# Latent attention: the queries' root mean square as a scale per row of the softmax, and steps of pairs in another order

## The reference, cut to what matters

```python
def _rmsnorm(x, g):
    y = x * lax.rsqrt(mean(x * x, axis=-1) + RMS_EPS)
    return y * g

def _mla_branch(x, w_in, q_norm, w_q_up, kv_norm, w_kv_up, w_out):
    h = x @ w_in                                   # 384 q, 256 kv, 32 rope, 1024 gate
    cq, ckv, k_rope, gate = split(h)
    q  = _rmsnorm(cq, q_norm) @ w_q_up             # 16 heads of 64 + 32 (rope)
    kv = _rmsnorm(ckv, kv_norm) @ w_kv_up          # 16 heads of 64 (k) + 64 (v)
    q_rope, k_rope = rope(q[..., 64:]), rope(k_rope)
    s = (q_full @ k_full.T) * 96 ** -0.5           # causal
    o = softmax(s) @ v
    return (o * silu(gate)) @ w_out

x = layernorm((2 * DEPTH) ** 0.25 * x + y)         # after each of the four layers
```

## Time and profile before

| What | Value |
|---|---|
| median of three runs | 1652.9 us (1652.37 to 1653.56) |
| profiled execution, its own time | 1657.83 us |
| its span, first to last instruction | 1656.0 us |
| mean granted TensorE clock | 0.995 |
| PE matmul busy | 1620.8 us (98%) |
| DVE, ACT, POOL busy | 776.0, 757.8, 658.2 us |
| share of PE in the chain that ended last | 80% |

### The profile page before, as it was taken

The page is one execution under the profiler, slowest core; times in us unless marked ns, Lnnn a source line. Parts: engine busy times, 40 slices in busy tenths (PEclk is TensorE's granted clock), DMA queues, the critical chain, the costliest instruction groups (busy, mean ns, idle before and its releaser), DMA issues.

```text
span 1656.0 us, 26230 instructions
## 1 busy us (share of the span) xinstructions
PE 1620.8 (98%) x10245; PEld 1313.5 (79%) x10245; DVE 776.0 (47%) x2044; ACT 757.8 (46%) x1465; POOL 658.2 (40%) x551
## 2 busy tenths in 40 slices
PE   8999999999999999999999999999999999999998
PEld 7777778887888787788777788777688888888877
DVE  3778635665543434354877464886051111001162
ACT  4566624655345444434576534328553322213252
POOL 5332234332443333243423243882235444444423
PEclk9999999999999999999999998999999999999999
DMA  6323144233452323153312265231243333333412
GB/s 174 71 45 87 52 161 125 80 83 60 160 157 55 85 56 93 58 194 79 88 41 75 73 184 152 79 90 56 90 135 102 102 91 101 102 92 97 120 62 89
DMA packets 216071, 161.32 MB, mean 97 GB/s; under 512 B 53763, under 2 KB 197155, under 8 KB 215948
## 3 DMA queue, kind: packets, MB, share of 16 engines
q1 hardware_dynamic: 205904, 130.21, 28.1%
q10 hardware_dynamic: 9820, 29.40, 5.7%
q0 software_dynamic: 224, 0.03, 0.1%
HBM read 148.32 MB, written 11.14 MB: 96 GB/s over the span
## 4 chain that ended last, share of the span: by engine, by line
PE 80%; DVE 11%; ACT 5%; issue 2%; POOL 2%; DMA 1%; SPq 0%; DVEq 0%; ACTq 0%; POOLq 0%
PE banks L532 40%; PE banks L483 8%; PE banks L485 7%; PE banks L484 7%; PE banks L772 4%; PE banks L716 4%; PE banks L614 4%; PE banks L758 3%; PE banks L738 1%; DVE banks L2354 1%; ACT AB L1512 1%; DVE banks L2343 1%; DVE AB L2356 1%; ACT w_hi L1382 1%; ACT G L1634 1%
## 5 line engine op out<-in xcount | busy, mean ns | idle before, releaser
L2856 POOL TENSOR_TENSOR w_lo<-w_raw,w_hi 128x512 fp32r<-128x512 f32 (+2 forms) x506 | 617.5, 1248 | 968.0 <-ACT w_hi L1382 967.7
L1382 ACT ACTIVATE w_hi<-w_raw 128x1024 fp32r<-128x1024 f32 (+4 forms) x254 | 249.8, 994 | 158.7 <-PE banks L485 102.0
L532 PE MATMUL banks<-XTh,w_hi 128*128 128x512 f32 (+5 forms) x1216 | 283.6, 375 | 7.2 <-DVE XTl L2316 3.0
L532 PE MATMUL banks<-XTl,w_hi 128*128 128x512 f32 (+5 forms) x1216 | 274.0, 367 | 0.0
L532 PE MATMUL banks<-XTh,w_lo 128*128 128x512 f32 (+5 forms) x1216 | 272.4, 367 | 0.0
L532 PEld LDWEIGHTS banks<-XTh,w_hi 128*128 128x128 f32 (+2 forms) x1216 | 209.0, 190 | 53.7 <-issue 8.3
L532 PEld LDWEIGHTS banks<-XTl,w_hi 128*128 128x128 f32 (+2 forms) x1216 | 212.7, 189 | 37.8
L532 PEld LDWEIGHTS banks<-XTh,w_lo 128*128 128x128 f32 (+2 forms) x1216 | 212.7, 189 | 37.4
L483 PE MATMUL banks<-w_hi,OTh 128*128 128x512 f32 (+1 forms) x448 | 172.8, 386 | 1.6 <-DVE QKl L2080 1.5
L484 PE MATMUL banks<-w_lo,OTh 128*128 128x512 f32 (+1 forms) x448 | 167.8, 375 | 0.0
L485 PE MATMUL banks<-w_hi,OTl 128*128 128x512 f32 (+1 forms) x448 | 167.7, 374 | 0.0
(11 more groups left out here) (222 smaller groups left out, 2209.6 us busy)
## 6 DMA issues: line engine op xcount, KB each, us to landing
w_raw<-in_w_gate_up_dram SPq DMA_DIRECT2D x44, 512.0 KB, 3.8
w_raw<-in_fox_w_in_dram SPq DMA_DIRECT2D x30, 512.0 KB, 4.1
w_raw<-in_mla_w_in_dram SPq DMA_DIRECT2D x26, 512.0 KB, 4.9
w_raw<-in_w_in_dram SPq DMA_DIRECT2D x24, 512.0 KB, 4.0
w_raw<-in_w_down_dram SPq DMA_DIRECT2D x22, 512.0 KB, 3.6
w_raw<-in_swa_w_in_dram SPq DMA_DIRECT2D x20, 512.0 KB, 3.8
w_raw<-in_mla_w_out_dram SPq DMA_DIRECT2D x16, 512.0 KB, 3.2
x_spill<-AB ACTq DMA_DIRECT2D x16, 512.0 KB, 2.8
```

Source lines behind the costliest of these rows:

```text
L532: mm = nc.tensor.matmul(o, wt[:, k, :], xt[:, k, lo:hi], start=first and n == 0 and k == 0, stop=last and n == 2 and k == nk - 1, skip_gro ...
L1382: nc.scalar.activation(view(w_hi, u, RING), view(w_raw, u, RAW), ACT.Copy).then_inc(hi_done, 1)
L2856: ins = pool.tensor_tensor(low[at], raw[at], high[at].bitcast(F32), ALU.subtract)
```

## The change

The latents of the queries are no longer normalised. ACT writes `OTh` straight from the tile with the gain as scale, DVE writes `OTl` straight from the tile; the squares are summed by PE per query row into 128 partitions by 4 columns (four matmuls whose stationary side is the sum of squares); root and reciprocal are taken of that small tile, and two tiles come of it, `q_up` (scale times inverse root) and `q_down` (its negative). Exp in latent pairs takes `q_up` as a pointer for its scale, and the negative maximum is multiplied by `q_down`. The reciprocal for keys and values moves ahead of the first gate on DVE. Beside that `between` gives other lists: in the `aug` pairs 0 to 5, and in the second block's pairs, whose condition `pairs[0].sel` was not met before, since the first of the four pairs has none; and the window layer gets `norm_last=(5,)`.

```diff
@@ class Pair
+                self.by_row = rope is not None
@@ PE, pair_attention
                 def step(i, n):
+                    if n == 5:
+                        scored.add(i)
                     if n % 2:
                         scores(i + 2, n // 2)
                     else:
@@ between(i)
                     if i == n_pairs - 2:
-                        return [0], {2: [2], 4: [4]}
+                        return [0], {1: [2], 2: [4]} if pairs[i].sel else {2: [2], 4: [4]}
                     if pairs[0].window:
                         return ([0], {3: [2, 1, 3]}) if i == 0 else ([0, 1, 3, 2], {})
-                    if pairs[0].sel and i >= 0:
+                    if pairs[-1].sel and i >= 0:
                         return [0, 1], {1: [2, 3], 3: [4]}
+                    if pairs[0].aug is not None and 0 <= i < n_pairs - 2:
+                        return [0, 1, 3, 2], {2: [4, 5]}
                     return list(range(5)), {}
@@ behind the tiles of a pair
-                    scores(i + 2, 2)
+                    if i not in scored:
+                        scores(i + 2, 2)
                     mix(i)
@@ PE, mla(j)
-                for i in range(4):
+                for i in range(3):
                     tile("c")
-                square_sum(0, 0, 3)
+                q_latents = c.g
+                tile("c")
+                o = begin()
+                pe.wait_ge(sq_sum, 2 * j + 1)
+                for t in range(T):
+                    mm = nc.tensor.matmul(o[:, 2 * t:2 * t + 2], SQ[0][:, t * P:(t + 1) * P], ones[:, 0:2], start=True, stop=True,
+                                          skip_group_check=True)
+                end(mm)
@@ ACT, exps
-                        ins = nc.scalar.activation(sc, sc, ACT.Exp, bias=nb[:, b, n0 + t:n0 + t + 1], scale=pr.scale,
+                        ins = nc.scalar.activation(sc, sc, ACT.Exp, bias=nb[:, b, n0 + t:n0 + t + 1],
+                                                   scale=q_up[:, t:t + 1] if pr.by_row else pr.scale,
@@ ACT, latent(i)
                     nc.scalar.activation(SQ[i], o[:, :], ACT.Square).then_inc(sq_done, 1)
-                    stored(nc.scalar.activation(G[:, 2 + i, :], o[:, :], ACT.Copy))
+                    if i < 3:
+                        nc.scalar.activation(OTh[:, i, :], o[:, :], ACT.Copy, scale=qg[:, j, i:i + 1]).then_inc(c_hi, 1)
+                    else:
+                        stored(nc.scalar.activation(G[:, 2 + i, :], o[:, :], ACT.Copy))
...
-                high_latents(0, 3)
@@ DVE, pair_attention
-                        if pr.sinks is None:
+                        if pr.by_row:
+                            ins = nc.vector.tensor_tensor(nb[:, b, ns], mx[:, b, ns], q_down[:, :], ALU.mult)
+                        elif pr.sinks is None:
@@ DVE, mla(j)
+                def query_latent(i):
+                    o = group()
+                    dve.wait_ge(c_hi, 5 * j + i + 1)
+                    stored(nc.vector.scalar_tensor_tensor(OTl[:, i, :], o[:, :], qg[:, j, i:i + 1], OTh[:, i, :].bitcast(F32),
+                                                          ALU.mult, ALU.subtract))
...
-                inverse_root(0, c.g)
-                scaled(0, 0, 3)
+                groups_stored(dve, c.g)
+                link(nc.vector.reciprocal(q_up[:, :], q_up[:, :]))
+                nc.vector.tensor_scalar(q_down[:, :], q_up[:, :], -MLA_SCALE, None, ALU.mult)
+                link(nc.vector.tensor_scalar(q_up[:, :], q_up[:, :], MLA_SCALE, None, ALU.mult))
...
-                root_at = c.g
+                groups_stored(dve, c.g)
+                link(nc.vector.reciprocal(DV[1], DV[1]))
                 gate(0)
                 gate_at[0] = c.g
-                inverse_root(1, root_at)
-                scaled(1, 3, 5)
@@ DVE, window layer
-            pair_attention(swa_pairs(), fill, norm_first=(-1,))
+            pair_attention(swa_pairs(), fill, norm_last=(5,), norm_first=(-1,))
```

More of the change, by code:

```diff
@@ L243, in build @@
         qg = sb("qg", [P, 2, 5])
+        q_up, q_down = sb("q_up", [P, T]), sb("q_down", [P, T])
         bf = sb("bf", [P, HEADS])
@@ L936, in mla @@
             def mla(j):
[L938 to L941, removed]
-                for i in range(4):
-                    tile("c")
-                square_sum(0, 0, 3)
+                for i in range(3):
+                    tile("c")
+                q_latents = c.g
[6 more added lines that the diff above has]
+                end(mm)
                 place[c.g] = 5
@@ L948, in mla @@
                 tile("krope")
-                square_sum(1, 3, 5)
+                o = begin()
+                pe.wait_ge(sq_sum, 2 * j + 2)
+                end(nc.tensor.matmul(o[:, :], ones[:, :], SQ[3], start=True, stop=True))
                 place[c.g] = 4
@@ L1726, in mla @@
                 c.g += 1
[L1727 removed]
+                root(DV[1], group()[:, :], KVR)
                 from_tmp(QKh[0:ROPE, 7, :], RA[0:ROPE, :])
@@ L2416, in mla @@
             def mla(j):
-                def inverse_root(n, g):
-                    groups_stored(dve, g)
-                    link(nc.vector.reciprocal(DV[n], DV[n]))
-                def scaled(n, lo, hi):
-                    for i in range(lo, hi):
-                        nc.vector.scalar_tensor_tensor(G[:, 2 + i, :], G[:, 2 + i, :], qg[:, j, i:i + 1], DV[n],
-                                                       ALU.mult, ALU.mult).then_inc(c_tmp, 1)
+                def query_latent(i):
[3 more added lines that the diff above has]
+                                                          ALU.mult, ALU.subtract))
                 def low_latent(i):
@@ L2436, in mla @@
                 hi_rope = {}
-                link(add_squares(1, 0))
+                for i in range(3):
+                    query_latent(i)
+                    if i == 1:
+                        link(add_squares(1, 0))
                 add_squares(2, 0).then_inc(sq_sum, 1)
-                c.g += 5
-                inverse_root(0, c.g)
-                scaled(0, 0, 3)
+                c.g += 2
+                groups_stored(dve, c.g)
+                link(nc.vector.reciprocal(q_up[:, :], q_up[:, :]))
+                nc.vector.tensor_scalar(q_down[:, :], q_up[:, :], -MLA_SCALE, None, ALU.mult)
+                link(nc.vector.tensor_scalar(q_up[:, :], q_up[:, :], MLA_SCALE, None, ALU.mult))
                 add_squares(4, 3).then_inc(sq_sum, 1)
@@ L2449, in mla @@
                     nc.vector.tensor_copy(QKl[ROPE * n:ROPE * n + ROPE, 7, :], QKl[0:ROPE, 7, :].bitcast(F32)).then_inc(kr_done, 1)
-                for i in range(3):
-                    low_latent(i)
                 c.g += 1
-                root_at = c.g
+                groups_stored(dve, c.g)
+                link(nc.vector.reciprocal(DV[1], DV[1]))
                 gate(0)
                 gate_at[0] = c.g
-                inverse_root(1, root_at)
-                scaled(1, 3, 5)
+                for i in range(3, 5):
+                    nc.vector.scalar_tensor_tensor(G[:, 2 + i, :], G[:, 2 + i, :], qg[:, j, i:i + 1], DV[1],
+                                                   ALU.mult, ALU.mult).then_inc(c_tmp, 1)
                 gate(1)
```

15 lines of the change are left out of this document (8 added, 7 removed).

## The result

The changed kernel took 1662.61 us (median of 5 runs, 1661.07 to 1669.08), the kernel before, on the same chip, 1652.7 (1652.37 to 1653.56). The ratio is 1.007, with a 95% interval of 1.0046 to 1.0094: 9.9 us slower. The forecast was slower, by 5.1 to 1658.0; the direction was right, but the size was half: the median is just above the likeliest case's own range (1655.5 to 1662) and within the wider one (1648 to 1663.5).

What follows compares the result with a forecast made beforehand. PE's matmuls, busy 98% of the span, were taken as the bound. The terms -3.5 + 0.2 + 1.5 - 0.6 + 5.1 + 2.4 gave +5.1, on the median of 1652.9 us 1658.0; range 1648 to 1663.5, 8 in 10.

Steps and rivals of the forecast that it cites:

- the likeliest case: Whole kernel slower, by the summed steps: 1658.0 us, own range 1655.5 to 1662; chance 56%.
- The prologue: Latent prologue, two layers: PE's waits for the gate's store and rope go or shrink, -1.75 us a layer, -3.5 in all.
- the sum of squares: Latent prologue: eight small matmuls replace two of 128x512, about 1.0 us against 0.9; +0.1 a layer, +0.2 in all.
- The pointer: Latent pairs: a second pointer adds 0.09 us an Exp, 0.37 a head, on the path at four places: +1.5 us.
- The window layer: Iteration 5: gate's store goes first, but the turn inside the tile waits for the later norm: -0.6 us, not -1.74.
- The `aug` pairs: Iterations 0 to 5: S2 straight behind T2 waits for S0's banks, 0.85 us net a pair, +5.1 in six.
- T2's saved wait: `aug` pairs: moving T2 behind six matmuls saves its wait for the copy, 0.27 us; each interrupted tile costs some 0.1.
- The second block: T2 later in pairs 0 and 1 delays ACT's queue and pair 2's mix: +2.4 us, from -3.2 to +3.5.
- A late T2 was handed on: Rival said it isn't, in `aug` pairs and second block: those gain 1.0 and 3.2, total 1646.3 us; chance 22%.
- The cancelling case: Rival: `aug` pairs cost, but the second block gains or its lateness is soaked up: +0.2, 1653.1 us; chance 22%.
- The clock: New pauses in `aug` pairs or ahead of pair 2's mix bring another half-rate stretch, 6.5 us: 1664.5; chance a twentieth.

Runs made afterwards that it cites:

- s2_behind: Changed kernel with old order in second block's pairs 0 and 1, aug DMAs issued ahead of the gate, S2 behind the last tile: 1647.45 us at equal clock.
- no_rel: Changed kernel with the second block's pairs in their old order: 1658.77 us at equal clock.
- latent_norm: Changed kernel with both orders of pairs (aug and second block) as before, latent part and window layer's norm as changed: 1649.49 us at equal clock.
- rel2_only: Changed kernel with old order in aug pairs and second block's pairs 0 and 1, only pair 2's turns in closer places: 1647.59 us at equal clock.

## Why the prediction was half right, step by step

- **The prologue**, -1.75 a layer and +0.1 for the sum of squares: -1.67 measured in all. Right, with the wait for the gate's store gone. The eight small matmuls took 0.80 where the two wide ones had taken 0.9, so they cost nothing.
- **The pointer**, +1.5: the price of one was right (0.093), the count of places was wrong. I counted waits of the low part that followed four Exps without a pause, two a layer; there were four places, 3.2 us. Two of them were no waits in the kernel before: ACT was just ahead there, and 0.37 a head was more than it had in hand.
- **The window layer**, -0.6: -0.88. The turn waited 0.77 and began at 394.55 in the trace after, which runs 0.64 early there: 395.2, against my 395.4.
- **The `aug` pairs**, +5.1: this is the step that failed, by 3.2 of the 4.5 between forecast and traces. "Net 1.03 - 0.27 + 0.1 = 0.85; six times" held to a hundredth in the pairs 0 and 3 (0.84, 0.81), and with the DMAs early in all six (0.81 to 0.88). What was missing is the sentence before it: I asked what S2 now waits for, and not what S2 had been covering in its old place. In four pairs S0 came 0.68 sooner behind the issue of the DMAs than before, and waited: 3.3 us. Pair 0 escapes since the iteration ahead of it still has its S2 as cover, pair 3 since the work of `values` stands between the mix ahead and its T0 (596.10 to 604 in the trace after). The claim that T2's saved wait is 0.17 a pair held too (s2_behind: 0.09 to 0.17).
- **The second block**, +2.4: 2.3 at equal clock (no_rel). ACT's queue carried the late T2, as forecast, though not where I put it: T0 of pairs 1 and 2 moved back by 0.4 and 1.7 only (1.1 and 3.0 forecast), and more came at T1 of pair 2, with 1.87 for a copy. In the profiled trace mixes 1 to 3 add 4.1, since the clock was down for 6.8 us about the wait, and 2.7 to 2.8 in the three traces where it was down for 3.4.
- **The rivals.** A late T2 was handed on in both places. The cancelling case was wrong as a sum, but its germ was right: pair 2's closer turns are worth 2.0 (1.5 of it by the clock), and only what pairs 0 and 1 hand on hides it. The clock had a twentieth; no trace has a stretch at 1.2 GHz in the `aug` pairs, for all their waits of 0.88. The long stretch near 1000 us, in two of five executions of the changed kernel by their mean clock, is in some of the kernel before as well.

Sum: -3.3 (prologues) + 3.2 - 0.9 + 8.3 + 2.3 = 9.6, against 8.4 measured. Part of the difference is the yardstick. The trace of the kernel before (1657.83), less the 7.3 us that its stretch near 1000 us costs (latent_norm, no_rel and rel2_only, without one, gain 7.29 to 7.35 there), stands for an execution of 1650.5, one of its faster group, while 1652.7 is of the slower. A sum of differences between traces is against the first. This is an estimate, since starts differ by a microsecond or so, and what parts the two groups isn't shown.

What stays open is the clock near 1000 us. The stretch at 1.2 GHz began between 998 and 1008 us in the eight traces that have it. Ahead of it PE waits 1.2 us for the low part of an activation, in the traces of both kernels. Executions with the lower mean clock took 6 to 9 us more; they were 50 of 123 with all kernels but the one before, and 9 of 83 of the kernel before. Whether the edits make it likelier, or the chip's state while they ran, the runs don't tell.

## What to carry to other kernels

Before a piece of work on the busiest engine is moved, ask two questions and not one: what will it wait for in its new place, and what did it cover in its old one, on every queue, DMAs included. A transfer that never shows a wait may have no slack at all. A price on an engine that is off the path is counted at every place where that engine is less than the price ahead, not only where somebody waits for it already.

## What the runs showed of the hardware

A second [128,1] pointer in an ACTIVATE adds 93 ns, about what the first does (805, 712 and 622 ns at 128x512 with two, one and none). Eight float32 matmuls with a full stationary tile and two moving columns take 0.80 us together, 0.10 each. And executions of one kernel differ by 6 to 9 us with their mean granted clock; in the traces one stretch of 13.5 us at half rate costs 7.3. A change of 0.3% can be read only between executions of the same granted clock, or from mix to mix within the traces, where stretches of equal code mostly agree to 0.05 us.
